# A two-layer decoder trunk on one core: the router turned round, result-free matmuls beside its waits, the first gather by token tile

## The reference, cut to what matters

```python
h2 = rmsnorm(x, ffn_norm[layer])
logits = jnp.einsum('bsd,de->bse', h, w_router)          # 256 x 1024 by 1024 x 8
top_v, top_i = lax.top_k(logits, 2)
top_w = jax.nn.softmax(top_v, axis=-1)
gate = jnp.sum(one_hot(top_i, 8) * top_w[..., None], axis=-2)
for e in range(8):                                       # d_ff 3584
    y = y + gate[..., e:e+1] * ((silu(h @ w1[e]) * (h @ w3[e])) @ w2[e])
x = x + y
```

## Time and profile before

| what | value |
|---|---|
| three runs | 1592.32, 1592.51, 1595.32 us (median 1592.51) |
| profiled execution | 1593.62 us, its span 1591.8 us |
| granted TensorE clock, mean over the span | 0.989 of 2.4 GHz |
| TensorE matmuls busy | 1549.4 us, 97% of the span |
| VectorE, ScalarE busy | 1267.9 us, 1052.8 us |
| DMA | 445.34 MB, mean 280 GB/s |
| end of the mixer to the first expert matmul | 534.5 to 560.86 us |
| 32 matmuls of the first gather, of the second | 7.07 us, 3.52 us |

### The profile page before, as it was taken

How to read it: one execution, slowest core, us unless ns; L and a number is a source line. 1 busy time by engine, 2 the same in 40 slices (tenths; PEclk the granted TensorE clock), 3 DMA queues, 4 the chain that set the end, 5 groups by cost and what they waited for, 6 DMA issues and landing times.

```text
span 1591.8 us, 23204 instructions
## 1 busy us (share of the span) xinstructions
PE 1549.4 (97%) x7253; PEld 1271.5 (80%) x7253; DVE 1267.9 (80%) x1329; ACT 1052.8 (66%) x1159; POOL 5.9 (0%) x12
## 2 busy tenths in 40 slices
PE   7999999999999899999999999999999999999997
PEld 6888888788888778878878878877887887887885
DVE  5885655446976679789789789789889979978978
ACT  6565544336564467677687687687778768767766
POOL 0000000000000000000000000000000000000000
PEclk9999999999999789999999999999999999999999
DMA  9444565358543679799899999999989989989985
GB/s 331 159 159 133 185 198 167 107 191 282 167 160 109 233 228 302 255 369 371 288 375 370 312 354 367 338 329 371 374 296 370 370 297 367 369 293 372 372 305 193
DMA packets 361372, 445.34 MB, mean 280 GB/s; under 512 B 17728, under 2 KB 272744, under 8 KB 361336
## 3 DMA queue, kind: packets, MB, share of 16 engines
q1 hardware_dynamic: 360768, 442.73, 82.1%
q0 software_dynamic: 480, 2.13, 0.4%
q10 hardware_dynamic: 88, 0.02, 0.0%
HBM read 443.76 MB, written 1.05 MB: 279 GB/s over the span
## 4 chain that ended last, share of the span: by engine, by line
PE 83%; DMA 4%; issue 4%; DVE 4%; ACT 3%; SPq 1%; DVEq 0%; ACTq 0%
PE bank L748 25%; PE bank L750 25%; PE bank L749 25%; DMA w_raw<-in_moe_w 4%; PE bank L1036 2%; ACT w_hi L450 2%; PE bank L1062 2%; DVE w_lo L1127 1%; SPq L351 1%; DVE hT_lo L1517 1%; PE bank L830 1%; PE bank L774 1%; ACT hT_hi L739 0%; DMA x_residual<-in_x 0%; PE bank L814 0%
## 5 line engine op out<-in xcount | busy, mean ns | idle before, releaser
L1127 DVE TENSOR_TENSOR w_lo<-w_raw,w_hi 128x1024 fp32r<-128x1024 f32 (+1 forms) x448 | 780.9, 1755 | 113.9 <-ACT w_hi L450 113.1
L450 ACT ACTIVATE w_hi<-w_raw 128x1024 fp32r<-128x1024 f32 (+1 forms) x448 | 663.9, 1492 | 160.2 <-PE bank L750 145.2
L748 PE MATMUL bank<-w_hi,hT_hi 128*128 128x512 f32 (+1 forms) x1424 | 568.4, 399 | 6.6 <-DVE hT_lo L1517 2.5
L750 PE MATMUL bank<-w_hi,hT_lo 128*128 128x512 f32 (+1 forms) x1424 | 555.6, 390 | 0.0
L749 PE MATMUL bank<-w_lo,hT_hi 128*128 128x512 f32 (+1 forms) x1424 | 554.4, 389 | 0.0
L748 PEld LDWEIGHTS bank<-w_hi,hT_hi 128*128 128x128 f32 x1424 | 269.3, 189 | 63.6 <-issue 6.7
L750 PEld LDWEIGHTS bank<-w_hi,hT_lo 128*128 128x128 f32 x1424 | 269.0, 189 | 56.7
L749 PEld LDWEIGHTS bank<-w_lo,hT_hi 128*128 128x128 f32 x1424 | 269.9, 190 | 50.8
L1122 DVE TENSOR_TENSOR w_lo<-w_raw,w_hi 128x2048 fp32r<-128x2048 f32 (+2 forms) x100 | 201.5, 2019 | 96.8 <-ACT w_hi L444 96.0
L444 ACT ACTIVATE w_hi<-w_raw 128x2048 fp32r<-128x2048 f32 (+2 forms) x100 | 169.6, 1699 | 161.1 <-PE bank L750 159.7
L748 PE MATMUL bank<-w_hi,hiddenM_hi 128*128 128x512 f32 x448 | 178.8, 399 | 1.1
(11 more groups left out here) (230 smaller groups left out, 1022.2 us busy)
## 6 DMA issues: line engine op xcount, KB each, us to landing
w_raw<-in_moe_w SPq DMA_DIRECT2D x448, 512.0 KB, 8.0
w_raw<-in_moe_w SPq DMA_DIRECT2D x448, 256.0 KB, 4.9
w_raw<-in_w_in SPq DMA_DIRECT2D x64, 512.0 KB, 4.6
w_raw<-in_dense_w SPq DMA_DIRECT2D x44, 512.0 KB, 4.8
w_raw<-in_dense_w SPq DMA_DIRECT2D x44, 256.0 KB, 2.8
w_raw<-in_w_out SPq DMA_DIRECT2D x16, 512.0 KB, 4.6
w_raw<-in_w_pool_proj SPq DMA_DIRECT2D x8, 512.0 KB, 4.5
w_raw<-in_w_attn_proj SPq DMA_DIRECT2D x8, 512.0 KB, 4.1
```

Source lines behind the costliest of these rows:

```text
L450: act.activation(whi[:, m % SLOTS, 0:n], raw8[m % 8][:, 0:n], ACT.Copy).then_inc(s_hi, 1)
L748: pe.matmul(dst, ahi, bhi, start=start, stop=False)
L750: return pe.matmul(dst, alo, bhi, start=False, stop=stop)
L1127: dve.tensor_tensor(wlo[:, m % SLOTS, 0:n], raw8[m % 8][:, 0:n], whi[:, m % SLOTS, 0:n], ALU.subtract).then_inc(s_lo, 1)
```

## The change

- Router: the 8 weight columns are stationary, 256 tokens move; 8 channel blocks x 3 = 24 matmuls into one bank, logits transposed (8 x 256). VectorE copies them out to a new tile (1 KB in each partition), two transposes bring them back to 128 x 8 in bank 5, and the factor of the norm is applied there.
- `norm(3)` on VectorE moves from before the router's wait to behind that copy. On ScalarE a Sqrt of one column into another new tile is added between the two pairs of `hT_hi` of the second layer.
- `keep_busy(n, b)`: n matmuls of 128 x 128 by 512 columns on data that lie in an attention tile, into bank b, whose result nobody reads. 4 after the mixer, 9 after the logits' transposes, 3 after the position products, 6 after the first gather.
- `rows_lo(1)` moves behind `select(0)`, and the first gather goes token tile by token tile, each waiting for its own half of `x_rows_lo`. A start flag stands only at the first matmul of each bank. The gathers inside the loop stay as they are.

```diff
@@ tiles @@
+        lgT = sb("router_logitsT", [E, S])
+        sq0 = sb("sqrt_first", [P, 1])
@@ scalar, layer @@
                 hT_hi(3 * l + 2, 16 + 8 * l, (0, 1))
                 if l == 0:
                     ahead(c + 25)
+                else:
+                    act.activation(sq0[:], cst[:, C_ONE:C_ONE + 1], ACT.Sqrt)
                 hT_hi(3 * l + 2, 16 + 8 * l, (2, 3))
                 norm(2 * l + 1)
@@ tensor @@
+            def keep_busy(n, b):
+
+                for _ in range(n):
+                    pe.matmul(bank[b][:], aThi[:, 0, 0:P], aThi[:, 0:2, :], start=True, stop=True)
+
             layer(1, LAYER1, first=lambda: x_T(2, 1))
+            keep_busy(4, 5)
             x_T(3, 1)
...
                 pe.wait_ge(s_tlo, 20 + j + 1)
                 for k in (2 * j, 2 * j + 1):
-                    for t in range(TT):
-                        ins = three(bank[4 + t][:, 0:E], hThi[:, k, t * P:t * P + P], hTlo[:, k, t * P:t * P + P],
-                                    wrhi[:, k, :], wrlo[:, k, :], k == 0, k == KC - 1)
+                    ins = three(bank[4][0:E, 0:S], wrhi[:, k, :], wrlo[:, k, :], hThi[:, k, :], hTlo[:, k, :],
+                                k == 0, k == KC - 1)
             ins.then_inc(s_rt, 1)
+            pe.wait_ge(s_lt, 1)
+            for t in range(TT):
+                ins = pe.transpose(bank[5][:, t * E:t * E + E], lgT[:, t * P:t * P + P], cst[0:E, C_ID:C_ID + E])
+            ins.then_inc(s_rl, 1)
+            keep_busy(9, 0)
             pe.wait_ge(s_mk, 1)
...
             pe.matmul(bank[7][:, 0:E], ones, tmp8[:, 1, :], start=False, stop=True).then_inc(s_pos, 1)
+            keep_busy(3, 0)
 
             def gather(i):
 
                 pe.wait_ge(s_sel, i + 1)
+                if isinstance(i, int):
+                    for t in range(TT):
+                        pe.wait_ge(s_xrl, t + 1)
+                        for j in range(2):
+                            for q in range(4):
+                                k = 4 * j + q
+                                for x in (xrhi, xrlo):
+                                    ins = pe.matmul(bank[2 + j][:, q * P:q * P + P], x[:, t, k * P:k * P + P],
+                                                    selR[:, t, :], start=(t == 0 and q == 0 and x is xrhi),
+                                                    stop=(t == TT - 1 and x is xrlo), skip_group_check=True)
+                            if t == TT - 1:
+                                ins.then_inc(s_g, 1)
+                    return
...
-            pe.wait_ge(s_xrl, 2)
             gather(0)
+            keep_busy(6, 0)
@@ vector @@
-                norm(2 * l + 1)
+                if l == 0:
+                    norm(1)
...
             dve.wait_ge(s_rt, 1)
+            dve.tensor_copy(lgT[:], bank[4][0:E, 0:S]).then_inc(s_lt, 1)
+            norm(3)
+            dve.wait_ge(s_rl, 1)
             for t in range(TT):
-                ins = dve.tensor_scalar(lg[:, t, :], bank[4 + t][:, 0:E], st[:, 3, t:t + 1], None, ALU.mult)
+                ins = dve.tensor_scalar(lg[:, t, :], bank[5][:, t * E:t * E + E], st[:, 3, t:t + 1], None, ALU.mult)
...
-            for t in range(TT):
+
+            def rows_lo(t):
+
                 dve.wait_ge(s_xr, t + 1)
                 dve.scalar_tensor_tensor(xrlo[:, t, :], X[:, t, :], st[:, 3, t:t + 1], xrhi[:, t, :],
                                          ALU.mult, ALU.subtract).then_inc(s_xrl, 1)
 
+            rows_lo(0)
             dve.wait_ge(s_pos, 1)
...
             select(0)
+            rows_lo(1)
```

More of the change, by code:

```diff
@@ L256, in build @@
         s_rt = sem("router_done")
+        s_lt = sem("router_logitsT_in_sbuf")
+        s_rl = sem("router_logits_done")
         s_gd = sem("gate_diff")
```

## The result

The changed kernel takes 1616.15 us in the median of four runs (1615.82 to 1617.24) and the kernel before 1592.41 (four runs, 1591.96 to 1595.32): a ratio of 1.0146 with a 95% interval of 1.0129 to 1.0164. That is 23.7 us slower, where 5 us faster was forecast.

What follows compares the result with a forecast made beforehand. TensorE was taken to bound the kernel, so an earlier expert start counts fully: 3.8 us from the earlier start plus 1.2 from fewer slow matmuls, 5.0 together, giving a 1587.5 us median, range 1582.5 to 1590.5.

Steps and rivals of the forecast that it cites:

- the expert stage's place in the sum: Expert stage: costs what its matmuls cost, weights being there; unchanged in length from its first warm matmul on.
- case S: Expert ring: new tiles move it and slow the weight stream; at 8% loss 12 us more, 1599; chance 0.03.
- The point from which it decides: Expert ring: moves 344 GB/s in a job, reaches about 370, so a slower stream matters from a 7% loss on.
- the ring: Expert ring: an earlier start might find chunks not there and give gain back; given nothing of its own.
- case B: Router to experts: clock falls near 546, first expert matmul 3.8 us earlier, 5.0 gained, 1587.5 us; chance 0.50.
- logits scaled: Router, end of norm: logits scaled at 542.1, 2.65 us gained so far, norm being later than the logits' transposes.
- mask at TensorE: Between logits and position matmuls: TensorE gets the mask at 545.0, after 2.88 us of unchanged work.
- gain of the stage: Router stage: 3.8 us from the earlier start and 1.2 from fewer slow expert matmuls, together 5.0.
- a fixed 2.88: Between logits and positions: the work is unchanged and takes 2.88 us, as in the kernel before.
- case A: Router to experts: the clock never falls, first expert matmul at 554.0, 9.5 us gained, 1583.0; chance 0.22.
- C: Router: transposes and router cannot hold the clock, which falls at 539.3 as before; 3.3 us gained, 1589.2; chance 0.13.
- D: Norm on ScalarE: Square not in Sqrt's table, a second load makes norm 1.9 later; 3.1 left, 1589.4; chance 0.07.

Runs made afterwards that it cites:

- run 1: The changed kernel with its two new tiles allocated behind all others, no instruction changed; 1588.43 us, ratio 0.9975 to the kernel before.
- run 4: The kernel of run 1 with four small tiles allocated ahead of the ring, so all eight slots start on multiples of 256 bytes; 1577.84 us, ratio 0.9906.
- run 3: The kernel before with four small tiles allocated ahead of the ring, so all eight slots start on multiples of 256 bytes; 1582.65 us, ratio 0.9938.
- run 6: The kernel of run 4 with 17, 6 and 12 result-free matmuls in place of 9, 3 and 6; 1574.29 us, ratio 0.9885.
- run 5: The kernel of run 1 without any of its 22 result-free matmuls; 1587.91 us, ratio 0.9975 to the kernel before.
- runs 7 and 8: 7: changed kernel, slots 4 to 7 moved to 64 bytes past a multiple of 256, 1611.59 us; 8: kernel before, those slots 32 past, 1620.38 us.
- run 9: The kernel of run 6 with GpSimd's three clears held back until the select is written; 1574.41 us, ratio 0.9882.

## Why the prediction was wrong

**The step that failed is the expert stage's place in the sum.** The sum adds nothing for it: the prediction says that the stage costs what its matmuls cost as long as its weights are there, and "They are". Measured, the stage became 27.6 us longer, because the two new tiles moved four of its eight raw slots and all its chunks then came at 348 GB/s. The prediction had this mechanism as case S, but gave it a chance of 0.03 and 12 us. Three things in that were wrong.

- "No row speaks for it." The DMA view of the trace of before speaks for it. I had read the mean, about 370 GB/s; in slices it is 385 and 348 in turns, four chunks each, and four is the number of slots in each of the two places. The three windows in the earlier trace rows that have a rate (380, 374, 46) do not show it. The stretch ahead of the experts shows it too: chunks 4 to 7 fill slots 4 to 7 first, then come slots 0 to 2. The kernel before, in those two stretches:

```profile
541.00:549.00 8.00, 5.08 (x25) 4.99 (x24) 4.75 (x21) 4.92 (x6) 2.12 (x3) 0.50 1.07 379
551.00:557.00 6.00, 5.69 (x27) 5.72 (x28) 2.64 (x19) 1.15 (x4) 0.00 (x0) 0.50 1.10 350
```

- The point from which it decides. I set the need at 344 GB/s, the mean over a job, and let the first 7% of a loss cost nothing. But the need isn't even: in the phase of full chunks TensorE takes 12 matmuls 0.228 us apart, 2.73 us, for 1.05 MB, which is 384 GB/s. At 348 a chunk takes 3.01, and the trace after shows ScalarE at that pace, from one chunk to the next 3.01, 3.04 and 2.99 us:

```profile
853.24 1.92 ACT L454 ACTIVATE w_hi<-w_raw 128x2048 fp32r<-128x2048 f32 x1 [0.80 <-DMA w_raw<-in_moe_w]
...
856.25 1.92 ACT L454 ACTIVATE w_hi<-w_raw 128x2048 fp32r<-128x2048 f32 x1
859.29 1.92 ACT L454 ACTIVATE w_hi<-w_raw 128x2048 fp32r<-128x2048 f32 x1 [1.12 <-DMA w_raw<-in_moe_w]
...
862.28 1.92 ACT L454 ACTIVATE w_hi<-w_raw 128x2048 fp32r<-128x2048 f32 x1 [0.25 <-DMA w_raw<-in_moe_w]
```

Over the 28 full chunks of a job the stream falls short by 28 x 0.28 = 7.8 us if all slots are slow, by half of it, 3.9, if four are, and by nothing if none is. The jobs take 130.8, 127.3 and 126.2: 4.6 and 1.1 over the last. What the ring holds when the phase begins covers about 3 us, an estimate from the differences 7.8 - 4.6 and 3.9 - 1.1. So the kernel before was already past the point from which the rate decides, and my threshold of 7% was no threshold.

- The view. The waits of TensorE in the earlier trace rows (8.9 and 1.0) were my evidence that it waits for nothing in a job. A lack of data shows there as matmuls a little further apart, not as idle time: busy time grew by 18.6 us in the same work. The waits of the engine that takes the chunks from the DMA were never asked.

My own sign for it was right and was the first thing seen after: "if it has grown, the ring or case S is at work".

**The rest, step by step.** It went as case B.

| step | predicted | measured |
|---|---|---|
| last of 24 router matmuls | 539.9 | 539.86, starts 0.115 apart |
| Sqrt on ScalarE | 540.85 | 541.27 |
| logits scaled | 542.1 | 542.69 |
| mask at TensorE | 545.0 | 544.92 |
| gather starts | 547.5 | 547.79 |
| clock falls, rises | near 546, 560.2 | about 545.7, 559.4 |
| first expert matmul | 557.05 | 557.20 |
| gain of the stage | 5.0 | 5.4 by `selectT`, 4.4 by run 1, 4.8 by run 4 less run 3 |

So the router stage went as forecast: its path, its waits and its clock. The logits come 0.6 late and the mask on time, so two terms were off and cancel, which is luck. GpSimd's clears wait for the router. Before, they ran beside a CAST; now they run beside norm's first step, which had 0.17 us in the earlier trace rows and takes 0.66. The stretch from logits to mask, which I took to be a fixed 2.88, is 2.23: in the kernel before it held that slow CAST, and the same step takes 0.17 after. Kernel before, then after:

```profile
545.82 0.82 DVE L1440 CAST router_index_f<-router_index 128x16 f32<-128x16 uint32 x1
```
```profile
543.76 0.17 DVE L1474 CAST router_index_f<-router_index 128x16 f32<-128x16 uint32 x1
```

Two small readings of the prediction were off and move nothing: in windows of 0.2 us the clock of the kernel before falls at 539.4, not 539.2, and 1 - 0.23/0.42 is 0.45.

**Cases A, C and D.** A did not come: the clock fell. But it was nearer than I thought, since 17 more result-free matmuls brought it (run 6 against run 4). C's premise does not hold: without any result-free matmul the clock stayed up through the router (run 5). D fell too: behind the early Sqrt no table load stands until the gates' at 555.91. By the Trainium skill (ScalarE: Activation LUTs, What ACT_TABLE_LOAD costs) a drain comes on top of each load. This trace does not show one: the moved load starts at 533.06, and its Sqrt 1.29 us later.

By the other rule that the prediction weighed, that of short idle gaps (TensorE: Matmul & The Clock Gate, Why this matters for your kernels, in the Trainium skill), case A would have come. The trace goes against it: the clock fell at about 545.7, with no idle time longer than 1.71 us ahead of it, among matmuls of 8 moving columns.

## What to carry to other kernels

A new tile, however small, moves all tiles allocated behind it: allocate it last, or compare the start addresses of the buffers that the DMAs fill, and put those on multiples of 256 bytes; here that alone gave 10 us of 1592. Read the DMA rate in slices and not as a mean, set it against the need of the hungriest phase, and ask the engine nearest to the DMA what it waits for. Result-free matmuls pay when they fill the waits up to the real work: too few and the clock falls anyway, and those that then run cold delay what stands behind them.

## What was not expected of the hardware

**Start address and DMA rate.** The full chunks, moved in packets of 1 KB (in the changed kernel 27.89 MB in 27918 packets between 680 and 760), came at 385 GB/s (run 3) into slots that start on a multiple of 256 bytes, and at 348 with starts 32, 64 or 128 bytes past one (runs 7 and 8, and slots 0 to 3 of before). The Trainium skill (DMA: Bandwidth & Descriptors, How a descriptor splits into AXI transactions) says that a descriptor is cut into pieces of 256 bytes, and that one which does not start on such a boundary begins with a piece from the boundary below, part of which is fetched and not used; it speaks of reads. The runs agree in the boundary of 256, here for the address that is written. That 32, 64 and 128 bytes past it cost the same, and the rates, are from the runs alone. Since no slot was tried at less than 32 bytes past or with sources moved, what inside the transfer takes the time is argued and not shown.

**GpSimd and VectorE.** Clears on GpSimd stretched a VectorE step that ran beside them: TENSOR_SCALAR of 128 x 2 from 0.15 (run 9) to 0.66 (after, run 6) and to 1.55 (run 1), and the CAST from 0.17 to 0.82. Steps a little later beside the same clears, RECIPROCAL and TENSOR_TENSOR, kept their 0.16 to 0.17. Each long step ends 0.03 us after a clear has ended: at 541.18 behind the first clear (to 541.15) in the changed kernel, at 540.82 behind the second (to 540.79) in run 1, and the CAST at 546.64 behind the second (to 546.61) before. So the step seems to be held until a running clear is over, and 0.66 or 1.55 is the rest of one clear or of two. Why it is one or two is open, and so is what makes a step one that is held: beside the third clear a TENSOR_SCALAR of 128 x 8 took its usual 0.24 in the kernel before (from 546.68), and one of 128 x 1 took 0.15 in run 9. That the clears are the cause was tested for the norm's step alone (run 9).

**Clock and shape.** 24 matmuls with 8 stationary and 256 moving columns, 0.115 us apart, kept the full clock where 48 with 8 moving columns lost it at 539.4 in the kernel before; run 5 shows it without any result-free matmul.
